# A new table of conditioning slabs for three closing stages, and eight filler products at the start

## What is computed

```python
for l in range(DEPTH):                                   # DEPTH = 2
    sh_m, sc_m, gt_m, sh_f, sc_f, gt_f = split(silu(c) @ w_mod[l] + b_mod[l], 6)
    ux = rmsnorm(x, g[0]) * (1 + sc_m) + sh_m
    mix_x = (fourier_and_attention(ux, ctx) @ att_w_out) if l == 0 else short_conv_mix(ux)
    x = x + gt_m * rmsnorm(mix_x, g[1])
    u = rmsnorm(x, g[2]) * (1 + sc_f) + sh_f
    x = x + gt_f * rmsnorm(square(relu(u @ w1[l])) @ w2[l], g[3])
```

## Time and profile before

| | us |
|---|---|
| median of 3 runs | 2288.25 (2282.03 to 2288.31) |
| profiled execution, whole | 2291.2 |
| its span, first to last instruction | 2289.4 |
| TensorE busy | 2221.3, 97% |
| VectorE busy | 1655.6, 72% |
| ScalarE busy | 1019.6, 45% |
| GpSimd busy | 98.5, 4% |
| share of the chain of waits on TensorE / VectorE / DMA | 84% / 6% / 4% |
| mean granted TensorE clock | 0.987 |
| read from HBM | 588.46 MB, 258 GB/s |

### The profile page before, as it was taken

How to read it: one execution, slowest core, us unless ns; L and a number is a source line. 1 busy time by engine, 2 the same in 40 slices (tenths; PEclk the granted TensorE clock), 3 DMA queues, 4 the chain that set the end, 5 groups by cost and what they waited for, 6 DMA issues and landing times.

```text
span 2289.4 us, 30993 instructions
## 1 busy us (share of the span) xinstructions
PE 2221.3 (97%) x11363; PEld 1817.7 (79%) x11363; DVE 1655.6 (72%) x1784; ACT 1019.6 (45%) x1269; POOL 98.5 (4%) x32
## 2 busy tenths in 40 slices
PE   6899999999999999999989999999999999999998
PEld 3478568788888888888868888877888888888887
DVE  0266767788788888888989888987887654655565
ACT  3163544554344335344454444445444443443443
POOL 0000000001010110110101101100011000000000
PEclk8899999999999999999999999999999999999999
DMA  9966978688888878879868888895887656666654
GB/s 365 345 228 224 373 263 303 208 276 275 300 283 280 294 261 293 289 272 313 297 202 279 269 300 273 274 311 168 295 283 251 204 191 191 187 197 193 204 190 150
DMA packets 253896, 592.63 MB, mean 259 GB/s; under 512 B 18082, under 2 KB 18610, under 8 KB 253234
## 3 DMA queue, kind: packets, MB, share of 16 engines
q1 hardware_dynamic: 253746, 590.63, 76.8%
HBM read 588.46 MB, written 2.10 MB: 258 GB/s over the span
## 4 chain that ended last, share of the span: by engine, by line
PE 84%; DVE 6%; DMA 4%; ACT 3%; issue 3%; SPq 0%; DVEq 0%; ACTq 0%
PE ps L523 29%; PE ps L524 14%; PE ps L586 11%; PE ps L587 11%; PE ps L588 11%; PE ps L550 2%; DVE wlo L1263 2%; DMA early<-in_w_mod_dram 2%; ACT whi L897 1%; DMA mraw<-in_w_mod_dram 1%; DVE acc L1273 1%; DMA raw<-in_mlp_w_dram 1%; PE ps L481 1%; DVE fq L1426 0%; PE ps L678 0%
## 5 line engine op out<-in xcount | busy, mean ns | idle before, releaser
L1263 DVE TENSOR_TENSOR wlo<-raw,whi 128x1024 fp32r<-128x1024 f32 x712 | 905.2, 1275 | 431.9 <-ACT whi L897 430.4
L897 ACT ACTIVATE whi<-raw 128x1024 fp32r<-128x1024 f32 x712 | 751.6, 1058 | 951.2 <-PE ps L588 380.8
L523 PE MATMUL ps<-u,whi 128*128 128x512 f32 x2944 | 1044.7, 400 | 12.7 <-DVE wlo L1263 9.4
L524 PE MATMUL ps<-u,wlo 128*128 128x256 f32 x2944 | 826.8, 281 | 0.0
L523 PEld LDWEIGHTS ps<-u,whi 128*128 128x128 f32 x2944 | 554.3, 188 | 158.3 <-DVE wlo L1263 11.2
L524 PEld LDWEIGHTS ps<-u,wlo 128*128 128x128 f32 x2944 | 557.1, 189 | 0.2
L586 PE MATMUL ps<-whi,h 128*128 128x512 f32 x1216 | 475.3, 391 | 4.2 <-DVE wlo L1263 4.2
L587 PE MATMUL ps<-wlo,h 128*128 128x512 f32 x1216 | 473.9, 390 | 0.0
L588 PE MATMUL ps<-whi,h 128*128 128x512 f32 x1216 | 473.6, 390 | 0.0
L1273 DVE SCALAR_TENSOR_TENSOR acc<-mraw,cs,acc 128x1024 f32<-128x1024 f32 x240 | 306.6, 1278 | 3.5 <-DMA mraw<-in_w_mod_dram 3.5
L586 PEld LDWEIGHTS ps<-whi,h 128*128 128x128 f32 x1216 | 228.7, 188 | 54.2 <-DVE wlo L1263 6.4
(11 more groups left out here) (195 smaller groups left out, 1268.6 us busy)
## 6 DMA issues: line engine op xcount, KB each, us to landing
raw<-in_mlp_w_dram SPq DMA_DIRECT2D x512, 512.0 KB, 4.7
mraw<-in_w_mod_dram SPq DMA_DIRECT2D x272, 512.0 KB, 5.5
early<-in_w_mod_dram SPq DMA_DIRECT2D x96, 512.0 KB, 6.6
raw<-in_conv_w_in_dram SPq DMA_DIRECT2D x96, 512.0 KB, 5.3
raw<-in_att_w_in_dram SPq DMA_DIRECT2D x40, 512.0 KB, 4.8
raw<-in_att_w_out_dram SPq DMA_DIRECT2D x32, 512.0 KB, 6.4
raw<-in_conv_w_out_dram SPq DMA_DIRECT2D x32, 512.0 KB, 5.9
raw<-in_w_mod_dram SPq DMA_DIRECT2D x16, 512.0 KB, 6.6
```

Of the source, the lines that this page charges most:

```text
L523: pe.matmul(bank, whi[:, s % SLOTS, cols], src[:, k, :], start=(k == 0), stop=False)
L524: last = pe.matmul(bank[:, 0:T], wlo[:, s % SLOTS, cols], src[:, k, 0:T], start=False, stop=(k == KC - 1))
L897: act.activation(whi[:, s, :], raw[:, s, :], ACT.Copy).then_inc(hi_ready, 1)
L1263: dve.tensor_tensor(wlo[:, s, :], raw[:, s, :], whi[:, s, :], ALU.subtract).then_inc(lo_ready, 1)
```

## The change

Two things are changed.

```diff
-UNIT_EARLY = ((0, ((0,), (1,), (), (2,), (), (3,), (4,), ())), (5, ((0,), (1,), (), (2,), (), (3,), (4,), ())),
-              (10, ((0,), (1,), (2,), (), (3,), (4,), (5,), ())), (16, ()))
+UNIT_EARLY = ((0, tuple((s,) for s in range(SL))), (8, tuple((s,) for s in range(SL))), (16, ()), (16, ()))
...
+            def keep_clock(bank, n, wide=512):
+
+                for _ in range(n):
+                    pe.matmul(ps[:, bank, 0:wide], ident, tab[:, 0:wide], start=True, stop=True)
+
...
             turn_rows(3)
+            keep_clock(7, 8, T)
             for s in range(SLOTS, SL):
                 first_group_slab(s)
...
-            def keep_clock(bank, n):
-
-                for _ in range(n):
-                    pe.matmul(ps[:, bank, :], ident, tab[:, 0:512], start=True, stop=True)
```

## The result

| | before | changed |
|---|---|---|
| median of 20 runs each, us | 2285.73 | 2292.51 |
| lowest to highest, us | 2280.02 to 2292.19 | 2287.26 to 2298.00 |
| profiled execution, us | 2291.2 | 2293.8 |

The ratio is 1.0026, 95% interval 1.0017 to 1.0035: by it the change costs 5.9 us (3.9 to 8.0); the two medians lie 6.8 apart. That is within the 0.3% (6.9 us) that I called no change, at its upper edge, and the interval reaches beyond it. 1.0 us was forecast, and the interval leaves that out. The two profiled executions lie only 2.6 us apart, since that of before was a long one.

What follows compares the result with a forecast made beforehand. TensorE, busy for 97% of the span, was taken to bound the kernel. −16.6 taken away, +17.9 of new waits and −0.3 for the filler make +1.0 us; from the median 2289.3, rounded 2290 us, range 2278 to 2298.

Steps and rivals of the forecast that it cites:

- What the change takes away: Closing stages: waits for column sums, late splits in M and lower clock in O and C all go, −16.6 us.
- rival (3): Third step in O and C: split of position 20 or 21 stays late, keeping some 3 us; 2293, chance 0.07.
- O: Closing stage, attention's output projection, 350 to 447 us: 4.2 us taken away, 3.2 us of new waits.
- M: Closing stage, last quarter of the first MLP, 1083 to 1176 us: 4.7 us taken away, 9.5 of new waits.
- C: Closing stage, convolution's output projection, 1463 to 1560 us: 7.7 us taken away, 5.2 us of new waits.
- What it brings in: First two steps of closing stages: VectorE's pitch exceeds TensorE's 2.72 us a position, new waits of +17.9 us.
- the loop: SyncE's in-order queue: accumulation, issue, landing, ScalarE copy and split close over three positions, 9.15 us, 3.05 a position.
- Besides working, VectorE waits: First two steps of closing stages: 0.43 us a position without work, taken from third steps' 0.36, 0.45 and 0.62.
- VectorE busy over 0.93 in the second steps: Sign that the +17.9 us is right: VectorE's busy share in the closing stages' second steps.
- rival (2): Positions 3 to 15, all three stages: queue decides, landings to 6.5 us, 26 us of waits; +10, 2298, chance 0.23.
- These waits should not lower the clock: New waits in closing stages leave 2.4 GHz; if the clock falls there, 1.7 us each time, the forecast is wrong.
- The filler: At the start, behind the last turned row: products raise the clock sooner, −0.3 us, at most 0.5 gained.

Runs made afterwards that it cites:

- filler_alone: The kernel before with the eight filler products added and the old table of conditioning slabs kept; 2286.2 us, ratio 0.9997.
- rows_late: The changed kernel with the two row loads of O and M issued behind the second step, their vector finished a step later; 2293.5 us, ratio 1.0024.
- old_in_m: The changed kernel with the old table (5, 5, 6) kept in M alone; 2288.3 us, ratio 1.0001.
- table_alone: The changed kernel without the filler behind the last turned row, the new table kept; 2290.5 us, ratio 1.0013.
- the new order: In the closing stages SyncE issues each conditioning slab one place later, behind the next weight slab; on the changed kernel (weight_first) ratio 0.9991.
- 6, 6, 4: The changed kernel with six accumulations in each of the first two steps and four at the third's head; 2285.0 us, ratio 0.9989.
- weight_first: The changed kernel with each conditioning slab issued one place later in the closing stages, behind the next weight slab; 2285.7 us, ratio 0.9991.
- six_weight_first: The changed kernel with table 6, 6, 4 and each conditioning slab issued one place later, row loads unmoved; 2271.2 us, ratio 0.9930.

## Why the prediction was right, and where it was not

**What the change takes away: right, to 0.7 us.** Forecast −4.2, −4.7, −7.7; the changed kernel won back 4.3, 5.2 and 7.8. What fell with it, rival (3): the third step keeps nothing. The size rests on the one trace of before; by filler_alone's, with the same old table, it would be 2.8 us more in O, 0.4 more in M and 2.1 less in C.

**What it brings in: right in kind, 4.4 us too small.** Forecast 3.2, 9.5, 5.2, measured 5.9, 10.9, 5.5. The waits end with the split, lie in the second steps of O and C and from position 6 on in M, half of them in M, in pieces of 0.2 to 3.3 us. ScalarE's copies wait for landings there, as I had said (15.9 us in nine waits in C from 1510 to 1539). The pitch of the splits was 3.51 in O (364.1 to 416.8 over 15), 3.51 in M behind the slow split, 3.22 in C, against 3.4, 3.4 and 3.27. C, where the loop and VectorE's work were all there was, is the stage that I had right. O and M have the two row loads besides, and the step that failed is **"Besides working, VectorE waits", the 0.43 us**: it was taken from third steps, which have no row loads, and carried to steps that have them. In the changed kernel the waiting was 0.54 us a position in O, 0.53 in M and 0.38 in C. rows_late shows the rows' own share by position 10, 1.3 us or more in O and 2.8 or more in M, where a late landing behind them costs a wait at once. It does not show that they are all of what the 0.43 lacked: over the whole of the two steps its pitch was 3.39 in O (364.8 to 415.6 over 15), 3.32 in M (1107.7 to 1154.2 over 14) and 3.29 in C (1492.3 to 1541.7 over 15), and since a moved vector takes 0.15 off the work a position in O and M, that is still a waiting of 0.56, 0.49 and 0.45. What sets the rest stays open. This is what to look for when work is moved: what else leaves by that queue.

**"VectorE busy over 0.93 in the second steps": wrong in O** (0.78), right in M (0.94 from 1131) and nearly in C (0.89). "DMA share above 0.95": only behind the row loads (1.00); else 0.86 to 0.94. Each resource had gaps while TensorE waited, which fits a loop in which each waits for the other in turn.

Two slips of the sum change nothing: C's work a position adds up to 2.83, not 2.84, and with landings of 6.5 us the loop of rival (2) is 3.5 a position, not 3.55, and its waits 24 us, not 26.

**The clock: right in this trace, not in the others.** "These waits should not lower the clock", said the prediction, and the sum had no term for it. No lower clock lies inside the three stages of the changed kernel's trace, but in six of the seven others with the new table (old_in_m counted, for O and C) it fell behind such waits, for 1.7 us lost (table_alone, in M) up to 5.1 (rows_late, in O and M). old_in_m, in O:

```profile
415.70:419.00 3.30, 2.74 (x7) 2.17 (x8) 3.27 (x6) 2.53 (x6) 0.00 (x0) 0.50 0.98 356
```

The old table has its own scatter: in filler_alone the clock was low for 6.9 us in O, 3.4 in M and 6.8 in C, in before for 3.4, 0 and 6.8. So neither side of the comparison is fixed by one trace.

**The filler: sign right, a little too small.** Forecast −0.3 with at most 0.5 to be gained; −0.7 in the changed kernel, 0.2 of it through the split that I had held fixed.

**The sum.** By the two traces the closing stages make +5.0, by table_alone +6.3; with the old table they make 0 and +1.1. The difference is about 5 us for the table; less 0.7 for the filler makes a little over +4, and the ratio says +5.9 (3.9 to 8.0). The forecast of no change held, by 1 us and with an interval that reaches past its edge; the size of +1.0 did not hold, since the new waits were 4.4 us too small in the sum and the two other terms together gave back only 1.1. Of the rivals, (2) had the right direction and a part of its marks: the mean pitch was 3.4, where it wanted 3.5, and landings beyond 6.5 us stand behind the row loads (up to 8.7) and at the end of the second steps (7.2 us for the slab issued at 412.8 in O, 7.7 for that of 1529.8 in C), not from position 3 on everywhere.

## What to carry to other kernels

Before moving side work into fewer steps, write down for each step everything that leaves by the same queue, not just the kind of work that is moved: two loads that I had not in mind made about a quarter of the new waits in M, and some in O. Where side work has a deadline, move no more of it than the deadline asks for: four accumulations left at the head of the third step met the deadline of the sums, and the pace was kept in O, with the new order in C too. And in a queue that is executed in order, put the load that the critical engine hangs on ahead of the one that may itself have to wait. The two go together: by the sums of the stages the new order brings 3.8 us with the table of sixteen in two steps and 9.4 with 6, 6, 4, and the table 6, 6, 4 brings 7.7 us with the old order and 13.3 with the new one.

## What the runs showed of the hardware

**TensorE has two rhythms at the same granted clock.** In the convolution's twelve groups the products alternate between 512 and 256 columns without a wait. Busy time by stretch of the same 200 us, before and then weight_first:

```profile
1240.00:1440.00 200.00, 200.00 (x1134) 173.34 (x1133) 176.07 (x184) 87.24 (x94) 15.04 (x4) 1.00 0.82 277
```
```profile
1240.00:1440.00 200.00, 200.00 (x1156) 176.59 (x1155) 178.99 (x191) 88.80 (x97) 16.17 (x4) 1.00 0.83 283
```

1134 products against 1156, at a clock of 1.00 in both. Start to start, a pair takes 353 ns in the one, in a pattern that repeats after three pairs (120, 235, 114, 232, 118, 241 ns), and 347 ns in the other (230, 117, over and over). The convolution kept one rhythm from its beginning to its end in all fourteen traces; it is 4.5 us shorter in the quick one, and a quarter of an MLP's first product 1.4. How much of the scatter between executions of one kernel this makes isn't shown, since each kernel was profiled once. The quick rhythm stood in the convolution in all four kernels of one chip and in six_weight_first on another, never in the seven on two further chips; what decides it stays open. It is why the table above leaves these stages out, and of the 16 us of six_weight_first up to 4.5 may be owed to it, if the kernel before did not have it on that chip.

**The same idle time, two clocks.** At the boundary behind M TensorE idles 2.5 us in both kernels, beside a split that takes 5.41 us under GpSimd's reduction. Changed kernel, then before:

```profile
1217.80:1221.20 3.40, 3.40 (x11) 2.91 (x12) 3.40 (x4) 0.00 (x0) 1.16 (x2) 0.50 0.66 164
```
```profile
1214.50:1218.00 3.50, 3.50 (x21) 3.04 (x22) 3.50 (x4) 0.00 (x0) 1.21 (x2) 1.00 0.67 160
```

The idle times are 2.48 and 2.52 us; the clock fell behind the shorter one. All fourteen kernels idle there, for 2.47 to 2.52 us before the same product; in nine of the traces the clock falls behind it for 3.4 us, in five it doesn't. So an idle time alone does not tell whether the clock falls, and a forecast should price such a fall by its chance.
